# Sparse attention: the rotation of the heads' halves by transfers of SyncE instead of matmuls

## What is computed

```python
def _rope(x, pos):
    d = x.shape[-1]
    half = d // 2
    inv_freq = ROPE_THETA_2 ** (-(jnp.arange(half, dtype=jnp.float32) * 2.0 / d))
    ang = pos.astype(jnp.float32)[..., None] * inv_freq
    cos = jnp.cos(ang)[:, :, None, :]
    sin = jnp.sin(ang)[:, :, None, :]
    xf = x.astype(jnp.float32)
    x1, x2 = xf[..., :half], xf[..., half:]
    out = jnp.concatenate([x1 * cos - x2 * sin, x2 * cos + x1 * sin], axis=-1)
    return out.astype(x.dtype)

def _dsa_mixer(h, positions, w_in, q_norm_g, k_norm_g, idx_k_ln_g, idx_k_ln_b, w_out):
    Bn, T, _ = h.shape
    proj = h @ w_in
...
    q = _rope(_rmsnorm(q, q_norm_g), positions)
    k = _rope(_rmsnorm(k, k_norm_g), positions)
    qi = _rope(qi, positions)
    ki = _rope(_layernorm(ki, idx_k_ln_g, idx_k_ln_b)[:, :, None, :], positions)[:, :, 0, :]
    wi = wi * (IDX_HEADS ** -0.5 * IDX_DIM ** -0.5)
...
        s = jnp.einsum('bqhd,bsd->bqhs', qib, ki)
        score = jnp.einsum('bqhs,bqh->bqs', jax.nn.relu(s), wib).astype(jnp.float32)
        causal = key_idx[None, :] <= t_idx[:, None]
        score = jnp.where(causal[None], score, -jnp.inf)
        _, sel = lax.top_k(score, topk)
...
        p = jax.nn.softmax(logits, axis=-1).astype(vg.dtype)
        o = jnp.einsum('bqgrk,bqkgd->bqgrd', p, vg)
```

## Time and profile before

| | |
|---|---|
| median of 3 runs | 2749.02 us (2748.1 to 2751.02) |
| profiled execution, its own time | 2748.04 us |
| its span in the profile | 2746.2 us |
| mean granted clock of TensorE | 0.992 |
| PE busy | 2686.3 us, 98% |
| PEld busy | 2182.4 us, 79% |
| DVE busy | 1325.6 us, 48% |
| ACT busy | 934.1 us, 34% |
| POOL busy | 769.7 us, 28% |

### The profile page before, as it was taken

One profiled execution on the slowest core, in us unless ns is written; L12 is line 12 of the kernel. 1 busy time (PEld: TensorE's weight loads), 2 busy tenths in 40 slices (PEclk: granted clock), 3 DMA queues, 4 the chain that ended last, 5 costly groups with the idle time before them and its releaser, 6 DMA issues.

```text
span 2746.2 us, 30698 instructions
## 1 busy us (share of the span) xinstructions
PE 2686.3 (98%) x12706; PEld 2182.4 (79%) x12706; DVE 1325.6 (48%) x1840; ACT 934.1 (34%) x1510; POOL 769.7 (28%) x627
## 2 busy tenths in 40 slices
PE   8999998999999999999999998999999999999999
PEld 7888886777777787888888665788888888888887
DVE  4344245655666544534524588463332554633323
ACT  4222233333544332422223344642222332422221
POOL 6563025554644577166700231000000000000000
PEclk9999999999999999999999999999999999999999
DMA  6543334433333355354533110123333323333332
GB/s 179 159 142 119 100 112 119 118 107 107 110 101 100 85 162 153 100 148 142 151 123 112 47 54 8 56 83 100 95 98 138 100 85 91 121 103 92 100 116 77
DMA packets 382300, 296.12 MB, mean 108 GB/s; under 512 B 15572, under 2 KB 335312, under 8 KB 382160
## 3 DMA queue, kind: packets, MB, share of 16 engines
q1 hardware_dynamic: 363632, 240.33, 29.7%
q0 software_dynamic: 16992, 52.25, 6.4%
q10 hardware_dynamic: 1536, 1.58, 0.2%
HBM read 290.40 MB, written 2.13 MB: 107 GB/s over the span
## 4 chain that ended last, share of the span: by engine, by line
PE 86%; DVE 9%; ACT 3%; POOL 1%; DMA 1%; issue 1%; SPq 0%; DVEq 0%; ACTq 0%; POOLq 0%
PE PS L380 17%; PE PS L381 17%; PE PS L383 15%; PE PS L458 7%; PE PS L459 7%; PE PS L460 7%; PE PS L385 2%; PE PS L417 1%; PE PS L419 1%; PE PS L418 1%; PE PS L886 1%; DVE WL L1585 1%; PE PS L586 1%; DVE TS L1585 1%; PE PS L611 1%; DVE SETS L1594 1%
## 5 line engine op out<-in xcount | busy, mean ns | idle before, releaser
L380 PE MATMUL PS<-HH,WH 128*128 128x512 f32 x2248 | 904.8, 402 | 0.1
L381 PE MATMUL PS<-HL,WH 128*128 128x512 f32 x2248 | 877.3, 390 | 0.0
L383 PE MATMUL PS<-HH,WL 128*128 128x512 f32 x1967 | 768.9, 391 | 0.0
L1585 DVE TENSOR_TENSOR WL<-RAW,WH 128x1024 fp32r<-128x1024 f32 (+1 forms) x306 | 399.5, 1308 | 502.0 <-ACT WH L977 501.4
L380 PEld LDWEIGHTS PS<-HH,WH 128*128 128x128 f32 x2248 | 424.0, 189 | 112.4 <-issue 27.9
L381 PEld LDWEIGHTS PS<-HL,WH 128*128 128x128 f32 x2248 | 424.3, 189 | 91.0 <-issue 6.5
L977 ACT ACTIVATE WH<-RAW 128x1024 fp32r<-128x1024 f32 (+1 forms) x318 | 330.2, 1040 | 358.8 <-PE PS L385 301.7
L383 PEld LDWEIGHTS PS<-HH,WL 128*128 128x128 f32 x1967 | 370.5, 188 | 78.9
L2397 POOL TENSOR_SCALAR ADA<-ADA,CA 128x512 f32<-128x512 f32 x168 | 302.5, 1801 | 10.2 <-DMA ADA<-in_ada_w 2.8
L2394 POOL TENSOR_TENSOR ASUM<-ASUM,ADA 128x512 f32<-128x512 f32 x168 | 233.8, 1391 | 14.0
L1585 DVE TENSOR_TENSOR WLr<-RAWD,WHr 128x1024 fp32r<-128x1024 f32 x82 | 101.3, 1236 | 257.8 <-ACT WHr L977 257.8
(11 more groups left out here) (346 smaller groups left out, 3341.5 us busy)
## 6 DMA issues: line engine op xcount, KB each, us to landing
ADA<-in_ada_w POOLq DMA_DIRECT2D x192, 256.0 KB, 3.2
RAW<-in_ffn_w_gate SPq DMA_DIRECT2D x88, 512.0 KB, 3.9
RAW<-in_ffn_w_up SPq DMA_DIRECT2D x88, 512.0 KB, 3.9
RAWD<-in_ffn_w_down SPq DMA_DIRECT2D x88, 512.0 KB, 3.6
RAW<-in_w_in SPq DMA_DIRECT2D x84, 512.0 KB, 3.9
RAW<-in_conv_w_in SPq DMA_DIRECT2D x24, 512.0 KB, 3.9
RAW<-in_attn_w_in SPq DMA_DIRECT2D x16, 512.0 KB, 3.8
RAW<-in_w_mlstm_branch SPq DMA_DIRECT2D x8, 512.0 KB, 4.0
```

Source lines behind the costliest of these rows:

```text
L380: pe.matmul(PS[:, b, :], wh[:, k, :], hi[:, k, :], start=k == 0, stop=False)
L381: pe.matmul(PS[:, b, :], wh[:, k, :], lo[:, k, :], start=False, stop=False)
L383: pe.matmul(PS[:, b, :], wl[:, k, :], hi[:, k, :], start=False, stop=False)
L1585: return v.tensor_tensor(out, x, y, op).then_inc(*tick("dve", *event))
```

## The change

The exchange of the halves moves from TensorE to SyncE. Four transfers for each tile (two for ki) copy blocks of 32 rows, crosswise, from the x buffer into a room in `TS`: slot 3 for tiles with an even number, slot 4 for odd ones, slot 5 for ki. SyncE's program does this ahead of fixed loads (`EXCHANGES`), after waiting for the tile, and for the `roped` of the tile that had the room before. The sign that was in the matrix now goes into the sines: ScalarE multiplies them once by -1 or 1 for each row (`C_SIGN`). VectorE's product reads the room and writes it, in place of reading PSUM. A rope has four `yield`s in all where it had two and a bank to wait for.

```diff
+C_SIGN = 258
...
-    for b in (0, 64):
-        for m in range(32):
-            c[b + m + 32, C_R2 + b + m] = -1.0
-            c[b + m, C_R2 + b + m + 32] = 1.0
+    c[:, C_SIGN] = np.where(i // 32 % 2, 1.0, -1.0)
...
+TILES = ([("ki",)] + [("qi", c) for c in range(4)] + [("v", 0), ("v", 1), ("k", 0), ("k", 1)]
+         + [("q", c) for c in range(8)])
+EXCHANGES = {DSA + 7: [("qi", 0), ("qi", 1)], DSA + 8: [("qi", 2)], DSA + 9: [("ki",), ("qi", 3)],
+             DSA + 12: [("k", 0)], DSA + 13: [("k", 1)]}
+EXCHANGES.update({DSA + 14 + c: [("q", c)] for c in range(6)})
+EXCHANGES[DSA + 20] = [("q", 6), ("q", 7)]
+def input_tile(m, key):
+    return (m["TS"][:, 0, :], m["TS"][:, 1, :], m["ADA"][:, 0, :], m["ADA"][:, 1, :])[TILES.index(key) % 4]
+def exchanged_tile(m, key):
+    return m["TS"][0:64, 5, :] if key == ("ki",) else m["TS"][:, 3 + key[1] % 2, :]
...
@@ tensor_program @@
-    def rope(j, source, key, n=P):
-        b = yield from behind.bank()
-        w.wait_ge(*at(*source))
-        clear(b)
-        pe.matmul(PS[0:n, b, :], C[0:n, C_R2:C_R2 + n], xs[j][0:n, :], start=True, stop=True).then_inc(*tick("pe", "rot", *key))
-        free[b] = ("turned", *key)
-        yield
-        behind.leave(b)
-        yield
+    def rope(j, key):
+        for _ in range(4):
+            yield
         held[j] = False
         known.add(key)
...
@@ scalar_program @@
         act(m["COS"], m["COS"], ACT.Sin)
-        act(m["SIN"], m["SIN"], ACT.Sin, "cs2")
+        act(m["SIN"], m["SIN"], ACT.Sin)
+        w.wait_ge(*here("act"))
+        act(m["SIN"], m["SIN"], ACT.Copy, "cs2", scale=C[:, C_SIGN:C_SIGN + 1])
...
@@ vector_program @@
     def rope(j, dst, key, n=P):
-        b = yield from behind.bank()
-        yield
-        ap = TS[0:n, 3 + ring["r"] % 2, :]
-        ring["r"] += 1
+        for _ in range(3):
+            yield
+        ap = exchanged_tile(m, key)
         w.wait_ge(*at("rot", *key))
         w.wait_ge(*at("cs2"))
-        done()
-        tt(ap, PS[0:n, b, :], sinT[0:n], ALU.mult, "turned", *key)
-        behind.leave(b)
+        tt(ap, ap, sinT[0:n], ALU.mult)
         yield
         w.wait_ge(*at("by cos", *key))
         done()
...
@@ sync_program @@
+    in_room = {}
+    def exchange(key):
+        out, x = exchanged_tile(m, key), input_tile(m, key)
+        room = "xch2" if key == ("ki",) else f"xch{key[1] % 2}"
+        source = {"ki": ("ki n",), "k": ("k n", key[-1])}.get(key[0], ("copied", *key))
+        w.wait_ge(*at(*source))
+        if room in in_room:
+            w.wait_ge(*at("roped", *in_room[room]))
+        in_room[room] = key
+        n = 2 if key == ("ki",) else 4
+        for r in range(n):
+            o = 32 * (r + 1 - 2 * (r % 2))
+            sp.dma_start(out[32 * r:32 * r + 32, :], x[o:o + 32, :]).then_inc(
+                *tick(room, *(("rot", *key) if r == n - 1 else ()), n=16))
+
     for j in range(3, CHUNKS):
+        for key in EXCHANGES.get(j, ()):
+            exchange(key)
         load(j)
```

More of the change, by code:

```diff
@@ L786, in index_key @@
             yield
-        yield from rope(j, ("ki n",), ("ki",), 64)
+        yield from rope(j, ("ki",))
         known.add("ki2")
@@ L817, in q_tile @@
         free[7] = ("rq read", c // 4)
-        yield from rope(j, ("copied", "q", c), ("q", c))
+        yield from rope(j, ("q", c))
     def k_tile(c, j):
@@ L832, in k_tile @@
             yield
-        yield from rope(j, ("k n", c), ("k", c))
+        yield from rope(j, ("k", c))
     def v_tile(c, j):
@@ L931, in tensor_program @@
         j = take_x() if c else first_qi
-        behind.work.append(rope(j, ("copied", "qi", c), ("qi", c)))
+        behind.work.append(rope(j, ("qi", c)))
     behind.work.append(indexer())
@@ L2089, in vector_program @@
     s2s = [TS[:, 2, :], m["S2"][:, :]]
-    ring = dict(x=0, s2=0, r=0, s=0)
+    ring = dict(x=0, s2=0, s=0)
     held = [False] * 4
@@ L2769, in build @@
         names = ["pe", "act", "dve", "pool", "c", "c2", "x0", "x1", "x2", "x3", "vs0", "vs1", "vs2", "vs3", "ib", "cs", "fm", "pos", "out",
-                 "ada0", "ada1", "rot0", "rot1", "row", "gp", "gn", "t0", "t1", "ga"] + [f"raw{i}" for i in range(NRAW)]
+                 "ada0", "ada1", "rot0", "rot1", "xch0", "xch1", "xch2", "row", "gp", "gn", "t0", "t1", "ga"] + [f"raw{i}" for i in range(NRAW)]
         sems = {n: ctx.enter_context(nc.semaphore(f"s_{n}")) for n in names}
```

## The result

The changed kernel takes 2758.56 us (median of 9 runs, 2754.66 to 2762.75), the kernel before 2748.45 us in the same comparison (9 runs, 2745.24 to 2754.76). The ratio is 1.0039, with a 95% interval of 1.0029 to 1.0049: 10.1 us slower. Beside three other kernels on another chip the same program came out at 2758.3 against 2749.8 us, 1.0033 (1.0021 to 1.0045). So it is slower by 0.3 to 0.4%; neither interval includes no change. The forecast was 2752.3, no measurable change; the range held the result, the likeliest case did not.

What follows compares the result with a forecast made beforehand. VectorE's list up to 1716 us was taken to set the pace, not TensorE. Terms -1.0 + 8.0 - 3.7 = +3.3 us on the profiled 2748.04 gave 2751.3, plus 1.0 to the median: 2752.3; range 2743.5 to 2759.5.

Steps and rivals of the forecast that it cites:

- the likeliest case: Whole kernel: the forecast itself, 2752.3 us, no measurable change; chance 0.50, and 0.52 for a time within 0.2%.
- The rival of TensorE as the bound: Whole kernel: TensorE is the bound throughout, all 15 matmuls come off, 16.5 us faster, 2732.5; chance 0.12.
- The handovers, 8.0 us lost: 1592 to 1652: VectorE waits 4.0 us after each KT addition (k 0/q 0, k 1/q 1) for transfers into the shared room.
- The index part, 1.0 us gained: 1536 to 1562: first index score at 1559.3 against 1561.84, 2.5 us gained, minus 1.5 for TensorE's half clock.
- nor for qi 2, whose handover is in the indexer's sum: Index part: qi 2's transfers also wait for a room just given back; counted in that part's 1.0 us gain.
- 1652 to 1681, 3.7 us gained: VectorE's waits of 2.72, 0.56 and 1.25 us shrink or go; 2.9 to 4.5 us to be had, middle taken.
- the signs: New profile: VectorE waits at KT and QI additions, TensorE idle before first index score, share below 98%, two smaller waits gone.
- VectorE's own work without those waits reaches that place at 1681.16 - 4.5: 1652 to 1681: with its waits gone, VectorE reaches the last rotation's place at 1676.7, its own work unchanged.
- VectorE's product reads SBUF in place of PSUM: 0.69 us for either kind: All ropes: VectorE's product takes 0.69 us from SBUF as from PSUM, so the new operand costs nothing.
- Behind 1681, nothing: 1681 to 1716, VectorE's stretch, and the attention pairs after: the forecast's sum has no term, 0 us.
- Late landings: At k 0/q 0 and k 1/q 1 landings take 4.9 us: 13.0 lost, +10.1 in all, 2759.1; chance 0.23.
- Handovers hidden: At the shared rooms: SyncE is ahead enough that VectorE never stands; 4.7 us gained, 2744.3; chance 0.15.

Runs made afterwards that it cites:

- changed_again: The changed kernel, unaltered, run again beside other variants on another chip: median 2758.30 us, 1.0033 to the kernel before.
- order_only: The kernel before, matmuls kept, with two more yields ahead of each rope, giving every engine the changed kernel's order: 2751.82 us, 1.0004 to before.
- operand: The kernel before, matmuls still made, but VectorE's products read the unrotated x buffer in SBUF in place of PSUM: 2753.12 us, 1.0016 to before.
- ki_first: The changed kernel with the index key's two transfers ahead of qi 2's four on SyncE: 2758.51 us, 1.0031 to the kernel before.
- k_rooms_again: The changed kernel with rooms of their own for k 0 and k 1 alone, second run: 2754.75 us, 1.0017 to the kernel before.
- rooms4_again: The changed kernel with four rooms in place of two, second run: 2747.68 us, 0.9996 to the kernel before.
- filler: The kernel with four rooms plus one f32 matmul of constants into an unread bank per q tile: 2747.13 us, 0.9992 to the kernel before.
- narrow: The kernel before with its 15 rotation matmuls cut from 512 columns to 2, waits and order kept: 2744.79 us, 0.9985 to before.

## Why the prediction was right or wrong

Executions differ in when the stage begins, so I measure from one row that all kernels have, ScalarE's copy of the index key's tile (1531.33 in before, 1529.90 in changed_again). The table gives the start of a row minus the start of that copy, in us; "down" is the first matmul of the next stage. changed_again, 2758.61 as profiled, lies at its median, so it stands for the changed kernel.

| row | before | order_only | operand | changed_again | ki_first | k_rooms_again | rooms4_again | filler |
|---|---|---|---|---|---|---|---|---|
| KI addition | 25.3 | 26.6 | 26.9 | 30.0 | 27.7 | 30.0 | 24.5 | 24.5 |
| first score | 30.5 | 31.8 | 33.6 | 34.3 | 32.0 | 34.3 | 27.5 | 27.5 |
| KT, k 0 | 86.2 | 87.8 | 89.2 | 90.2 | 89.1 | 90.4 | 83.3 | 83.3 |
| first PRE | 120.8 | 125.1 | 125.0 | 132.3 | 132.1 | 128.7 | 121.7 | 122.1 |
| first F | 152.4 | 159.6 | 156.7 | 163.1 | 163.0 | 159.7 | 152.7 | 153.2 |
| last mask | 184.1 | 191.4 | 192.0 | 198.5 | 198.6 | 195.4 | 188.2 | 188.5 |
| down | 249.6 | 256.8 | 257.5 | 264.0 | 264.0 | 260.8 | 253.7 | 253.9 |

One thing first. Against the one trace of before the stage is 14.4 us longer, the median only 8.5. The same gap of 4.5 to 5.2 us shows in the three kernels built from before: order_only +7.3 in the stage and +2.1 in the median, operand +7.9 and +3.4, narrow +0.5 and -4.3. So the profiled execution of before probably had its stage some 5 us quicker than is usual. Against changed_again it lost 3.8 us outside the stage: its copy stands at 1531.33 where changed_again has 1529.90, and from "down" to the end it takes 965.4 us where changed_again takes 962.9. Where in the stage these 5 us lie cannot be told from one trace, and two traces of the kernel with four rooms differ by 2.4 us in the stage as well. Differences among the other columns don't suffer from that.

**What bounds the kernel: right up to 1681.** VectorE's list, not TensorE, set the pace in the middle of the stage: from k 0's KT addition to the first PRE its only waits in the changed kernel are the two handovers. The rival of TensorE as the bound (16.5 us faster) is refuted twice, by narrow and by filler. Behind the first F it is VectorE's list alone in before (0.7 us of waits for TensorE up to the last mask), but not with the products in SBUF (4.4 us in operand).

**The handovers, 8.0 us lost: right as waits, too dear as a price.** The two waits are 3.97 and 3.92 us, in the place and by the chain that the order told. By the Trainium skill, page "DMA: Bandwidth & Descriptors", the table of the two cost components, one was an estimated 3.8, and the trace agrees. Undoing them gave 3.6 us by the medians, 3.2 in the table. The step that failed is "There VectorE has no slack, so both count in full": it has none, but standing still it is out of GpSimd's way. The forecast also left the KT addition at 0.69 us; GpSimd's operations fall beside it now, and it took 2.80.

**The index part, 1.0 us gained: wrong.** The first score came 3.8 us later than in before, and k 0's KT addition 4.1. Two steps of it failed. The key's transfers landed at 1560.2 instead of 1557.5: room 0 came free 1.6 us later, 0.4 of it because the reciprocal began later and most of the rest because the first QI addition was itself stretched beside GpSimd (two took 2.61 us, not 1.4); the issues took 0.6 each, and the last landing was longer than 2.4. And of the 12 weight matmuls that moved ahead of the first score only six ran ahead of TensorE's stop, the last of their tile, up to 1555.3. The other six are the next tile's, and needed a PSUM bank; ScalarE frees it by copying qi 3 into the key's x buffer, which is free when the key is roped. So TensorE stopped in front of these six for 7.17 us, and they came after the stop, at half clock:

```profile
1562.48:1565.48 3.00, 3.00 (x8) 1.96 (x10) 0.00 (x0) 2.23 (x3) 2.12 (x1) 0.50 0.29 70
```

From 1562.48 to the first score at 1565.30 are 2.8 us for six matmuls, which the forecast had put before 1556.4 at 1.3 us. The half clock itself was foreseen (1.5 us). Four rooms took away 6.7 us of this part (34.3 to 27.5 in the table), and with them the stop fell from 7.2 to 1.9: this is the larger part of the loss. The forecast had it in one clause, "nor for qi 2, whose handover is in the indexer's sum".

**1652 to 1681, 3.7 us gained: wrong.** The two smaller waits went, as the signs said (1.2 us of waits for TensorE are left), but from the first PRE to the first F the changed kernel takes 30.8 us and before took 31.5: 0.7 gained. The step that failed is that VectorE's own work stays as long as it was: "VectorE's own work without those waits reaches that place at 1681.16 - 4.5". In the profiled execution of the changed kernel these 31.0 us hold 28.33 busy us, in before 31.5 us held 25.49:

```profile
1664.90:1695.90 31.00, 22.01 (x119) 17.23 (x120) 28.33 (x70) 13.20 (x31) 9.38 (x5) 0.89 0.20 60
```

Nearly all of it is two additions into QT that now fall beside GpSimd, 1.74 and 2.37 us where they took 0.69 each. The second one, in before, in the changed kernel and in order_only:

```profile
1668.40 0.69 DVE L1585 TENSOR_TENSOR QT<-QT,TS 128x512 f32<-128x512 f32 x1
```

```profile
1680.60 2.37 DVE L1595 TENSOR_TENSOR QT<-QT,TS 128x512 f32<-128x512 f32 x1
```

```profile
1672.59 2.26 DVE L1589 TENSOR_TENSOR QT<-QT,TS 128x512 f32<-128x512 f32 x1
```

In order_only the products read PSUM, and the two additions take 1.60 and 2.26 us all the same. So this comes with the new order, and not with the product's operand, by these traces. The missing matmuls are worth little here by themselves: narrow takes 31.0 us.

**"VectorE's product reads SBUF in place of PSUM: 0.69 us for either kind": wrong.** That was read from rows where GpSimd was still. The change of operand costs 3.4 us by the median of operand, and was in the forecast at nothing.

**Behind 1681, nothing: 3.7 us lost, and open.** From the first F to the last mask, VectorE takes 31.7 to 31.8 us in before, narrow and order_only, and 35.2 to 35.8 in all eleven traces of kernels whose products read SBUF, operand among them. In these TensorE stays at half clock longer. Before, then order_only (its first and third piece), then changed_again, in 5 us pieces from the first F on:

```profile
1683.71:1688.71 5.00, 2.40 (x15) 1.52 (x14) 4.79 (x13) 1.52 (x4) 0.00 (x0) 0.84 0.00 0
1688.71:1693.71 5.00, 3.46 (x9) 1.59 (x9) 4.05 (x15) 1.84 (x6) 0.00 (x0) 0.50 0.00 0
1693.71:1698.71 5.00, 5.00 (x39) 3.85 (x38) 4.72 (x20) 3.81 (x12) 0.00 (x0) 0.96 0.01 2
```

```profile
1687.78:1692.78 5.00, 3.50 (x14) 2.70 (x14) 4.79 (x13) 1.52 (x4) 0.00 (x0) 0.53 0.00 0
...
1697.78:1702.78 5.00, 5.00 (x39) 3.95 (x38) 4.72 (x19) 3.74 (x12) 0.00 (x0) 0.94 0.00 2
```

```profile
1692.95:1697.95 5.00, 3.50 (x14) 2.70 (x14) 4.79 (x13) 1.52 (x4) 0.00 (x0) 0.50 0.00 0
1697.95:1702.95 5.00, 3.47 (x9) 1.60 (x9) 4.05 (x15) 1.84 (x6) 0.00 (x0) 0.50 0.00 0
1702.95:1707.95 5.00, 5.00 (x26) 4.45 (x26) 3.15 (x13) 2.05 (x7) 0.00 (x0) 0.50 0.00 0
```

In the third piece TensorE is as busy in all three, at 0.96, 0.94 and 0.50, and VectorE does 4.72 us of work in the first two and 3.15 in the last, waiting for scores. What makes the clock come back late is not settled. It is not the order and not TensorE's work in the first piece: order_only has both as in changed_again (3.50 us, 14 matmuls). It is not the missing matmuls: with the filler TensorE was busy for 1.42 of the 5 us ahead of the first F, as in order_only (1.46), and the stretch stayed long. What the eleven traces share and the other three lack is the product on SBUF, and no product stands in this stretch; by what way it would act was not tried, and most kernels have one trace.

**The sum.** By the table the parts are +4.1 to k 0, +7.3 from there to the first PRE (7.9 of waits), -0.7 and +3.7, together 14.4, where the forecast had -1.0, +8.0, -3.7 and 0. About 5 us of the 14.4 are probably owed to the one trace of before. The forecast's +3.3 was 5 to 7 us short of the medians. The terms that were too low are the index part (by 5.1 in the table), 1652 to 1681 (by 3.0) and behind 1681 (by 3.7); from k 0 to the first PRE it was 0.7 too high.

**The rivals.** "Late landings" gave 2759.1, next to the result, and is refuted nevertheless: the median landing is 2.0 us and the two handovers 3.9, not 6.5. Its number was reached by other terms. The range reached up to 2759.5 for this rival, so it was luck that it held the result. "Handovers hidden" is refuted by the waits. Of the signs, those for the handovers, for qi 2 (3.18 us, 3.5 foretold) and TensorE's share below 98% came. The late first pair came too, but not by the few microseconds foretold: the last mask stands at 1731.45, 15 us behind 1716. And the idle TensorE, expected in front of the first index score, stood in front of weight matmuls instead.

**What the exchange by transfers is worth here.** With rooms enough it is level with the matmuls, -0.3 and -2.1 us with intervals that include no difference. That it does not gain fits the two prices found from before: the matmuls had cost 4.3, and the product in SBUF costs 3.4.

## What to carry to other kernels

When work moves off the engine with the highest busy share, ask of each piece who waits for it: here three quarters of the 16.5 us of matmuls taken away were worth nothing, while a shared buffer, given back just before its next use, cost 10.6 us. A wait is not priced by following only the engine that waits: follow the buffers that the late tile holds, since the largest stop (7.17 us) stood on an engine that had nothing to do with the transfer. And before an operand moves from PSUM to SBUF, look at what GpSimd does beside it: price it from rows that overlap with GpSimd's, not from those that stand alone.

## What was not expected of the hardware

- A VectorE product of 128 x 512 with one operand in PSUM took 0.69 us beside a GpSimd operation in all 17 such rows of before, narrow and order_only; with both in SBUF it took 1.78 in the same place, ending half a microsecond after GpSimd's.
- Taking 7.9 us of waits from VectorE raised its busy time for the same instructions by 4.2 us (32.23 to 36.45), so that its busy time is no fixed amount of work.
- Transfers of 32 rows by 512 columns from SBUF to SBUF landed after 1.9 to 3.8 us, 2.0 in the median, and SyncE issued four in 2.41 us at most places; ScalarE's rows had made one expect 2.4 us and 0.54 each.
- VectorE's same 97 instructions, from the first F to the last mask, took 31.7 or 35.5 us, with the granted clock back to full some 10 us after the first F, or 18.
